# Row 0's transposes and logits taken behind the last two blocks of output products, in a two-layer mixer and mixture-of-experts kernel

## What is computed

```python
def reference(x, ...):
    for l in range(DEPTH):
        mix = hybrid_mixer(x, w_in[l], w_ret_o[l], w_dsa_o[l], w_out[l])     # ends: merged @ w_out
        h = layer_norm(DEEPNORM_ALPHA * x + mix, ln1_g[l], ln1_b[l])
        ffn = hierarchical_moe(h, router_grp_w[l], ...)   # logits = h @ router weights, top-1, top-2
        x = layer_norm(DEEPNORM_ALPHA * h + ffn, ln2_g[l], ln2_b[l])
    return x
```

## Time and profile before

| | us |
|---|---|
| median of 3 runs | 1721.98 |
| lowest and highest | 1720.21, 1722.23 |
| the profiled execution's own time | 1721.21 |
| its span, first to last instruction | 1719.3 |

### The profile page before, as it was taken

One profiled execution on the slowest core, in us unless ns is written; L12 is line 12 of the kernel. 1 busy time (PEld: TensorE's weight loads), 2 busy tenths in 40 slices (PEclk: granted clock), 3 DMA queues, 4 the chain that ended last, 5 costly groups with the idle time before them and its releaser, 6 DMA issues. The chain is left out here.

```text
span 1719.3 us, 21965 instructions
## 1 busy us (share of the span) xinstructions
PE 1391.8 (81%) x8566; PEld 948.5 (55%) x8566; DVE 617.3 (36%) x1068; ACT 398.1 (23%) x442; POOL 0.2 (0%) x4
## 2 busy tenths in 40 slices
PE   4999999998667757766779999999987576667656
PEld 3998789985223313322369987899843133223313
DVE  2788676653000000000157885875520000000003
ACT  2333644322010000101223346333211001010100
POOL 0000000000000000000000000000000000000000
PEclk8999999998888788878879999999997789778878
DMA  5555445598999999999915553365979999999994
GB/s 195 189 193 196 148 144 204 196 365 320 403 419 416 416 421 417 416 419 420 386 63 183 189 203 114 135 246 200 411 307 417 419 418 416 418 420 416 416 420 182
DMA packets 132402, 527.59 MB, mean 307 GB/s; under 512 B 7536, under 2 KB 11888, under 8 KB 99440
## 3 DMA queue, kind: packets, MB, share of 16 engines
q1 hardware_dynamic: 130192, 519.66, 76.4%
q10 hardware_dynamic: 2144, 6.99, 1.0%
HBM read 525.58 MB, written 1.05 MB: 306 GB/s over the span
## 5 line engine op out<-in xcount | busy, mean ns | idle before, releaser
L750 PE MATMUL psum<-ring,aqT 128*32 128x512 f32 x1984 | 342.9, 841 | 254.6 <-PEq L742 254.6
L750 PEld LDWEIGHTS psum<-ring,aqT 128*32 128x32 f32 x1984 | 91.0, 147 | 498.8 <-issue 498.8
L1266 DVE TENSOR_TENSOR w_low<-ring,w_high 128x2048 fp32r<-128x2048 f32 (+2 forms) x112 | 248.7, 2260 | 109.3 <-DVEq L1265 107.2
L917 ACT ACTIVATE w_high<-ring 128x2048 fp32r<-128x2048 f32 (+2 forms) x112 | 205.9, 1887 | 211.3 <-ACTq L914 203.2
L1481 DVE TENSOR_TENSOR qk<-psum,qk 128x512 f32<-128x512 f32 x16 | 11.1, 691 | 461.0 <-DVEq L1480 461.0
L485 PE MATMUL psum<-w_high,x_high 128*128 128x512 f32 (+2 forms) x384 | 152.2, 396 | 25.3 <-PEq L465 25.3
L717 PEld LDWEIGHTS psum<-aqT,h 128*128 128x128 f32 x576 | 138.8, 335 | 24.3 <-issue 24.3
L717 PE MATMUL psum<-aqT,h 128*128 128x128 f32 x576 | 142.8, 412 | 9.6 <-PEq L789 7.4
L485 PE MATMUL psum<-w_high,x_low 128*128 128x512 f32 (+2 forms) x384 | 150.2, 391 | 0.0
L485 PE MATMUL psum<-w_low,x_high 128*128 128x512 f32 (+2 forms) x384 | 149.7, 390 | 0.0
L505 PE MATMUL psum<-x_high,w_high 128*128 128x256 f32 x512 | 146.8, 287 | 0.0
(11 more groups left out here) (211 smaller groups left out, 1662.9 us busy)
## 6 DMA issues: line engine op xcount, KB each, us to landing
ring<-in_w_gate_dram SPq DMA_DIRECT2D x124, 1024.0 KB, 15.7
ring<-in_w_up_dram SPq DMA_DIRECT2D x124, 1024.0 KB, 19.5
ring<-in_w_down_dram SPq DMA_DIRECT2D x118, 1024.0 KB, 18.4
ring<-in_w_in_dram SPq DMA_DIRECT2D x36, 2048.0 KB, 8.0
ring<-in_w_ret_o_dram SPq DMA_DIRECT2D x8, 2048.0 KB, 8.4
ring<-in_w_dsa_o_dram SPq DMA_DIRECT2D x4, 2048.0 KB, 8.4
ring<-in_w_out_dram SPq DMA_DIRECT2D x4, 2048.0 KB, 7.7
spare<-in_w_up_dram SPq DMA_DIRECT2D x4, 1024.0 KB, 10.6
```

The lines of the kernel that those rows point to most:

```text
L750: mm = nc.tensor.matmul(bank[s, :], lhs[:, c, s], w[:, k, n * NB:(n + 1) * NB], start=(c == 0), stop=(c == chunks - 1))
L917: nc.scalar.activation(half_tile(high, to, w, b), half_tile(ring, i % RAW, w, b), ACT.Copy).then_inc(high_ready, 1)
L1266: V.tensor_tensor(half_tile(low, i % RAW, w, b), half_tile(ring, i % RAW, w, b), half_tile(high, of, w, b).bitcast(f32), ALU.subtract).the ...
```

## The change

TensorE runs the two last blocks of products (row 1, half 1) right behind the other six and takes HT0 and row 0's logits behind them. VectorE takes `choose(0)` behind both sums of row 1 instead of between them.

```diff
@@ -577,15 +577,15 @@
                 out_block(banks, 0, 1, 1)
                 out_block(banks, 1, 0, 1)
 
+                out_block(banks, 1, 1, 0, began=out_used[0, 1])
+                out_block(banks, 1, 1, 1, began=out_used[1, 0])
+
                 ps = begin("HT0")
                 pe.wait_ge(y_ready, 2)
                 turn_sums(0, range(KC), ps)
-                out_block(banks, 1, 1, 0, began=out_used[0, 1])
-
                 rl = begin("RL")
                 copied("HT0", "RL")
                 logits(0, range(KC), rl)
-                out_block(banks, 1, 1, 1, began=out_used[1, 0])
 
                 ps = begin("HT1")
                 for half in range(2):
@@ -1604,9 +1604,9 @@
                 V.tensor_scalar(h[:, 0, :], x[:, 0, :], mv[:, 0, 0:1], rstd[:, 0:1], ALU.subtract,
                                 ALU.mult).then_inc(xn_ready, 1)
                 add_up(1, 0)
-                choose(0)
                 add_up(1, 1)
                 free("OUT1")
+                choose(0)
                 moments(1)
                 root_guess(slice(1, 2))
                 root_steps(slice(1, 2), 1)
```

## The result

| | before | changed |
|---|---|---|
| median | 1721.98 us | 1728.55 us |
| lowest and highest of 7 runs | 1720.21, 1723.47 | 1727.73, 1729.56 |
| the profiled execution's own time, its span | 1721.21, 1719.3 | 1729.42, 1727.5 |

The changed kernel is slower: ratio 1.0038, 95% interval 1.0028 to 1.0049, or 6.6 us (4.8 to 8.4). The forecast was 4.4 us, the range 1724.0 to 1730.0 held the time.

The account below looks back on a forecast made before the run. The weight stream was taken to pace the expert loop, so only the seam ahead of it could move. The gather of row 0 comes 2.18 us later in each of 2 layers: 1721.98 + 4.4 = 1726.4 us, range 1724.0 to 1730.0.

Parts of the forecast that it names:

- Steps 1 to 4: At the seam: products end 2.6 us sooner, then HT0, uncovered copy, logits and choose(0) come late; pick ends at 388.30.
- Step 4: VectorE: moments(1), guess, root step, places(0) and pick, 1.87 us, queue behind choose(0); the products' 2.6 us are lost.
- Step 5: TensorE is free 0.18 us ahead of the pick, so the gather of row 0 starts 2.18 us later.
- the upper bound of a layer: Largest cost per layer: 2.6 us with slower hand-overs, 3.3 with row 1's logits at the low clock.
- rival C: First 32 expert matmuls run at 1.2 GHz: 1.97 us more per layer, 1730.3, or 1728.4 in one layer; chance 0.16.
- The reading of what bounds the kernel: The weight stream paces the expert loop; only its start, the seam ending at about 400 us in layer 1, can move.
- load 21: SyncE's weight load at 399.78, waiting for the first 32 expert matmuls; claimed to set the seam and move by 2.18.
- Step 6 and 7: Behind row 0's gather lengths stay, so row 1's gather, experts and load 21 move 2.18; other moved SyncE loads stay hidden.
- own signs of being wrong: moments(1) soon after add_up(1,1), load 21 keeping its time, or first expert matmuls taking over 4 us.
- A: Rival: delay absorbed because the first quad's landing, not TensorE, sets the seam; 0 per layer, 1722.0; chance 0.10.
- B: Rival: tile halves return sooner, loads 8 to 11 go sooner, 0.8 to 2.6 us gained per layer, 1717 to 1720; chance 0.04.

Follow-up runs that it names:

- e1: Kernel before with VectorE's half of the change alone, choose(0) behind both sums of row 1, TensorE's order as before: +5.5 us, ratio 1.0038.
- e3: Changed kernel with moments(1), the root and row 1's scale ahead of choose(0) on VectorE: +6.0 us over before, ratio 1.0035.
- e2: Changed kernel with VectorE's old order, choose(0) back between the sums, so TensorE's half of the change alone: +9.5 us over before, ratio 1.0058.
- e5: Changed kernel with useless matmuls cut to fit inside TensorE's two holes, ahead of row 0's logits and the counting matmul: +4.6 us over before, ratio 1.0029.
- e6: Kernel before with 3 useless matmuls on TensorE right ahead of the gather of row 0: +3.5 us, ratio 1.0022.
- e7: Kernel before with 3 useless matmuls (2.6 us) behind the gathers, right ahead of the first expert matmul: +0.2 us, ratio 1.0003.
- e8: Kernel before with 7 useless matmuls (6.0 us) behind the gathers, right ahead of the first expert matmul: +4.5 us, ratio 1.0028.
- e9: Changed kernel with moments(1) and root ahead of choose(0), and row 1's logits ahead of TensorE's wait for the choice: +4.8 us over before, ratio 1.0028.
- e10: Kernel before with the two loads of the second normalization's parameters moved from ScalarE to SyncE: -5.2 us, ratio 0.9971.
- e4: Changed kernel with 2 and 3 useless matmuls in TensorE's two holes, too long for them: +6.1 us over before, ratio 1.0038.

## Why the prediction was right, and where not

The time lay in the range, and the mechanism (a late choice, and TensorE and VectorE queued behind it) is the one that acts. The forecast of 4.4 us lies below the interval of the measured 6.6 (4.8 to 8.4): one term was priced at nothing.

*Steps 1 to 4* (the row-0 chain and VectorE's order) were right to a tenth of a us. HT0 was to start 5.60 after its old place; it did, within 0.01 (380.67 - 375.08). The copy, the logits and the choice followed as worked out: the choice's first operation at 26.77 from the first product matmul, by the sum 26.74. The hand-over from ScalarE to TensorE, bounded by 0.05 and 0.3, was 0.06 (381.83 + 1.02 = 382.85, logits at 382.91). e1 shows that VectorE's order alone is enough for a cost of this size. Step 4's reading, that moments(1) and places(0) behind the choice are what makes the gather late, is half of it: e3 took moments(1) out of that queue, and the gather stayed.

*Step 5* (TensorE free 0.18 us ahead of the pick) is the one that failed. At the high clock it was 0.13 us too late. Of the 0.31 us between the two, the hand-overs are 0.03 (choice to counting 0.15 for 0.12) and 0.10 (first counting matmul to logits 0.15 for 0.05), the logits 0.08 (1.78 to the gather for 1.70), and the pick came 0.10 sooner behind the choice's end (1.80 for 1.90). The term became 2.23 to 2.27 and not 2.18. The larger miss is the clock: I had put the price of a low clock in those logits at none, with 0.74 as the bound, by the ratio of the expert matmuls. It was 1.65 (3.60 - 1.95), a factor of 1.85, in one layer of the changed kernel's trace and in five of the six layers of e1, e2 and e3, in one of them in part (2.45). With it the sum is 2 x 2.23 + 1.65 = 6.1 for 6.6 measured. So the step that failed is a term of the sum that was mis-sized: the clock's price in row 1's logits, put at none, was 1.65 us in one layer. The prediction had the case, but only in the upper bound of a layer; its sum took none, and rival C put the slow stretch at the expert matmuls.

The Trainium skill (TensorE: Matmul & The Clock Gate, LDWEIGHTS) let me expect no cost, since it gives a weight load as 128 / 1.2 = 107 ns without regard to the granted clock. Here the measurement decides against it, at the low clock and, for the length of one load, at the high one too: 192 ns, though they follow each other at 0.11 us. Weight loads of the row-1 logits in the changed kernel, first in layer 1, then in layer 2 (duration in ns, least, median, most):

```profile
L559 PEld LDWEIGHTS psum<-sig,x_xT x16: 186/192/192, 387.6 to 389.3; 128*128 128x128 f32 x16
```
```profile
L559 PEld LDWEIGHTS psum<-sig,x_xT x16: 285/333/333, 1240.8 to 1243.9; 128*128 128x128 f32 x16
```

They slow down with the clock. The gathers were no fit model: their loads, a median of 335 or 336 ns at either clock, are as slow at 2.4 GHz as the logits' at 1.2 GHz. The same page's rule (Part 1: The HAM clock gate) that the low clock is the default and activity releases it agrees with the trace as far as the changed kernel's layer 2 and e5 go: the fall came inside the hole (0.82, then 0.50), and with the holes filled (e5) the logits ran at the high clock in both layers. A hole doesn't set the moment alone: in layer 1 of the changed kernel the same hole passed at 1.00, and in layer 1 of e1 the fall came inside the logits (0.76 over them).

*The reading of what bounds the kernel* was half right. That the seam's delay comes out at the end one to one is shown by e6. That load 21 carries it is wrong (e7, e8), and that the sum came out all the same is luck, since the chain which does carry it starts at the gathers too: behind the gathers TensorE has 3.6 to 3.8 us to give, and the chain through VectorE and ScalarE starts the loop. The prediction followed the loads up to load 21 and stopped there; what ended TensorE's wait between 399.78 and the loop's first load was not asked.

*Step 6 and 7* held for the gather of row 1, which keeps its distance (0.77 and 0.78 us of waiting), and for the first expert matmul, 2.3 us later in layer 1. They did not hold for load 21, 4.6 us later there for 2.18. Of the prediction's own signs of being wrong one came, first expert matmuls of over 4 us (5.92 in layer 1): it stood for rival C, and cost nothing because of the wait at L789, which the prediction hadn't seen. The later loads 12, 13, 19 and 20 cost nothing that the traces show.

*The rivals.* A (absorbed) didn't come for the gathers, but its mechanism exists one step further back. B (earlier loads help) didn't come: e2, which has the earlier blocks too, is the slowest of all. C came in layer 1, and was free behind a wait of 3.8 us.

Open: 1.14 us between the seams of the profiled execution, in a stretch without any change. From the second gather of layer 1 to the first product matmul of layer 2 the thirteen traces have 792.6 to 794.5 us, so it differs by as much between kernels that are equal there.

## What to carry to other kernels

When one late result is waited for by two engines, price both queues behind it: each may end within a tenth of a microsecond of the other, and then a gain on one alone doesn't show (e3), while a gain on both does (e9). A hole that a reordering opened on TensorE cost, in one of two layers here, the clock of what followed as well; filling it with useless matmuls that fit gave back about 2 us of 6.6. Before saying that a late load delays everything, delay just that load by a known amount: 2.6 us ahead of the first expert matmuls in each layer cost nothing that could be measured, 6.0 cost 4.5 in all, and the difference is a wait that was worth 5 us once it was removed (e10).

## What the runs showed of the hardware

- 16 matmuls of 40 float32 columns with 128-column weight loads take 1.95 us at a granted clock of 1.00 and 3.60 at 0.50; 16 gather matmuls of 128 columns take 4.15 at 0.50 and 4.05 at 1.00 (e4, e5; 3.84 behind the fillers of e6). These are records of the trace, two for each float32 matmul. The length of one weight load, median: 192 ns at 1.00 and 333 at 0.50 for the logits, 335 and 336 for the gathers, whose weights are read with a step of 8 elements.
- A granted clock that falls within a hole of 1.7 us (changed kernel, layer 2): 1.00 up to 1239.0, 0.82 over the 1.6 us of the hole, 0.50 behind it. The kernel before has its fall at the first gather instead, with no hole over 0.46 us ahead of it (0.78 over that gather, 0.50 over the next).
- The same kernel has the low clock at different places in its two layers (changed kernel: the expert matmuls in layer 1, the logits in layer 2), so one layer's trace is no sample of the other.
